# Early stores, roots and loads in a two-sequence encoder kernel, with six of eight gating products per up pair on GpSimd

## The reference, cut to what matters

```python
x = x + 0.5 * swiglu(rmsnorm(x, norm_ffn1), w_ffn1_gate, w_ffn1_up, w_ffn1_down)
x = x + hybrid_mixer(rmsnorm(x, norm_mix), ...)      # attention and gated linear attention
x = x + 0.5 * swiglu(rmsnorm(x, norm_ffn2), w_ffn2_gate, w_ffn2_up, w_ffn2_down)
y = rmsnorm(x, norm_final)

def swiglu(h, w_gate, w_up, w_down):
    return (silu(h @ w_gate) * (h @ w_up)) @ w_down
```

## Time and profile before

| | us |
|---|---|
| median of 3 runs (2459.72 to 2462.23) | 2461.09 |
| the profiled execution | 2464.09 |
| its span, first to last instruction | 2462.3 |
| TensorE busy in it | 2320.7 (94%) |
| VectorE busy | 1190.6 (48%) |
| ScalarE busy | 727.8 (30%) |
| GpSimd busy | 254.1 (10%) |
| mean granted TensorE clock | 0.974 |

### The profile page before, as it was taken

One profiled execution on the slowest core, in us unless ns is written; L12 is line 12 of the kernel. 1 busy time (PEld: TensorE's weight loads), 2 busy tenths in 40 slices (PEclk: granted clock), 3 DMA queues, 4 the chain that ended last, 5 costly groups with the idle time before them and its releaser, 6 DMA issues. The chain is left out here.

```text
span 2462.3 us, 32516 instructions
## 1 busy us (share of the span) xinstructions
PE 2320.7 (94%) x12960; PEld 2011.8 (82%) x12960; DVE 1190.6 (48%) x2022; ACT 727.8 (30%) x1366; POOL 254.1 (10%) x188
## 2 busy tenths in 40 slices
PE   3998999999989999999999889999999999999998
PEld 3998999999968877777778778888888888877887
DVE  5555555555546585856555674511111111136576
ACT  5322222222233344644443211311111111123343
POOL 5000000000000001111001222211111121100000
PEclk7999999999999999999999999999999999999999
DMA  3133222222286565422425824122222222246555
GB/s 121 35 99 100 72 72 73 86 76 72 87 304 219 178 195 151 145 96 83 134 80 171 277 108 159 35 80 81 79 74 72 104 78 89 74 147 198 188 177 174
DMA packets 227191, 298.08 MB, mean 121 GB/s; under 512 B 22880, under 2 KB 141664, under 8 KB 227040
## 3 DMA queue, kind: packets, MB, share of 16 engines
q1 hardware_dynamic: 216672, 275.01, 34.8%
q10 hardware_dynamic: 10368, 20.98, 2.3%
HBM read 205.49 MB, written 87.16 MB: 119 GB/s over the span
## 5 line engine op out<-in xcount | busy, mean ns | idle before, releaser
L1963 PE MATMUL ps<-h_hi,w_hi 128*128 128x512 f32 (+1 forms) x1488 | 536.4, 361 | 5.3 <-ACT q_rot L1139 2.5
L1964 PE MATMUL ps<-h_lo,w_hi 128*128 128x512 f32 (+1 forms) x1488 | 528.7, 355 | 0.0
L1965 PE MATMUL ps<-h_hi,w_lo 128*128 128x512 f32 (+1 forms) x1488 | 528.5, 355 | 0.0
L2030 PE MATMUL ps<-hs,w_hi 128*128 128x384 f32 (+1 forms) x1232 | 391.3, 318 | 50.5 <-DVE u L1530 42.9
L2031 PE MATMUL ps<-hs,w_hi 128*128 128x384 f32 (+1 forms) x1232 | 389.0, 316 | 0.0
L1963 PEld LDWEIGHTS ps<-h_hi,w_hi 128*128 128x128 f32 x1488 | 282.6, 190 | 65.0 <-issue 18.7
L2040 PE MATMUL ps<-w_hi,dh 128*128 128x512 f32 x770 | 304.0, 395 | 18.3 <-DVE w_lo L1596 11.8
L1965 PEld LDWEIGHTS ps<-h_hi,w_lo 128*128 128x128 f32 x1488 | 282.6, 190 | 39.9
L1964 PEld LDWEIGHTS ps<-h_lo,w_hi 128*128 128x128 f32 x1488 | 283.0, 190 | 37.6
L2032 PE MATMUL ps<-hs,w_lo 128*128 128x384 f32 (+1 forms) x992 | 313.0, 316 | 0.0
L2042 PE MATMUL ps<-w_hi,dh 128*128 128x512 f32 x770 | 302.6, 393 | 0.0
(11 more groups left out here) (210 smaller groups left out, 2858.9 us busy)
## 6 DMA issues: line engine op xcount, KB each, us to landing
dr<-hid_mid SPq DMA_DIRECT2D x154, 320.0 KB, 3.1
w_raw<-in_w_ffn_down SPq DMA_DIRECT2D x176, 256.0 KB, 3.4
hid_mid<-st SPq DMA_DIRECT2D x88, 320.0 KB, 3.5
w_raw<-in_w_ffn_gate SPq DMA_DIRECT2D x44, 512.0 KB, 4.0
w_raw<-in_w_ffn_up SPq DMA_DIRECT2D x44, 512.0 KB, 4.8
hid_mid<-sg SPq DMA_DIRECT2D x66, 320.0 KB, 2.6
w_raw<-in_w_in SPq DMA_DIRECT2D x14, 512.0 KB, 4.7
proj<-stage ACTq DMA_DIRECT2D x24, 256.0 KB, 3.2
```

The lines of the kernel that those rows point to most:

```text
L1963: mm(out, hi, rhs_hi, start=first, stop=False)
L1964: mm(out, hi, rhs_lo, start=False, stop=False)
L1965: return mm(out, lo, rhs_hi, start=False, stop=last)
L2030: mm(out, hi[:, k, :], b_hi, start=k == 0 and j in (GP1, GP6, GP5), stop=False, skip_group_check=True)
```

## The change

- GpSimd's order at the start: the roots of tiles 0, 1 and 2, then the splits of tile t followed by the roots of tile t + 3.
- In the up pair, the products for GP5, GP4 and GP3 (six of eight) are made by GpSimd (`g_gate`), with a semaphore of their own; GP2's two, which read PSUM, stay on VectorE.
- SyncE stores each of the three sg blocks when its product is made, behind the two weight loads of that iteration, and each of the four sums when it is made. Two semaphores count them. The SiLU waits for the sg stores and for the making of the sums; the next sums wait for the stores of the sums.
- At the end of gate/up the last four sums come before the last `d_prepare` on VectorE, and SyncE loads a hidden and a weight block for the down stage before the last stores. The same in the second FFN.
- The x tiles are reloaded in every second step, and the gain row later.
- `keep_p1` stands ahead of `d_hi` of the same step on ScalarE. `share_p1` moves to the last five steps of DP2.
- Some semaphores are merged, with counts to match (A2 silu and prod into S, masking into masked).

```diff
@@ -111,7 +111,8 @@
...
-G_MULT = numbered(e for e in GORDER if e[0] % NP in G_OUT and e[0] // NP % 2 == 1)
+G_MULT = numbered(e for e in GORDER if e[0] % NP == GP2 and e[0] // NP % 2 == 1)
+G_GATED = numbered(e for e in GORDER if e[0] % NP in G_OUT[1:] and e[0] // NP % 2 == 1)
@@ -505,16 +506,29 @@
...
-            def store_hidden(f, i):
-                sp.wait_ge(hid_summed, 4 * (GROUPS * f + i + 1))
-                for p, block in ((DP1, hid(f, 0)), (DP2, hid(f, 1)), (DP4, hid(f, 3)), (DP5, ST[f][:, 0, :]),
-                                 (DP6, ST[f][:, 1, :]), (DP7, ST[f][:, 2, :]), (DP3, ST[f][:, 3, :])):
-                    sp.dma_start(hid_mid[p, i], block).then_inc(hid_stored, 16)
+            def store_block(f, i, p, q):
+                sp.dma_start(hid_mid[p, i], hid(f, q)).then_inc(hid_stored, 16)
+
+            def store_hidden(i):
+                up = NP * (2 * i + 1)
+                for p, q, j in ((DP1, 0, GP2), (DP4, 3, GP5), (DP2, 1, GP4)):
+                    if j == GP2:
+                        sp.wait_ge(S["mult"], G_MULT[(up + j, 1)])
+                    else:
+                        sp.wait_ge(S["gated"], G_GATED[(up + j, 1)])
+                    store_block(0, i, p, q)
+
+            def store_sums(f, i):
+                for j, p in enumerate((DP5, DP6, DP7, DP3)):
+                    sp.wait_ge(hid_summed, 4 * (GROUPS * f + i) + j + 1)
+                    sp.dma_start(hid_mid[p, i], ST[f][:, j, :]).then_inc(sums_stored, 16)
 
             def load_hidden(f, n):
                 p, i = divmod(n, GROUPS)
-                if p == 0:
-                    sp.wait_ge(hid_stored, 16 * NP * (GROUPS * f + i + 1))
+                if p in (DP1, DP2, DP4):
+                    sp.wait_ge(hid_stored, 48 * (GROUPS * f + i + 1))
+                else:
+                    sp.wait_ge(sums_stored, 64 * (GROUPS * f + i + 1))
                 if n >= D_HID:
                     sp.wait_ge(W["a_lo"], D_STEPS * f + n - D_HID + 1)
                 sp.dma_start(DR[f][n % D_HID][:, :], hid_mid[p, i]).then_inc(hid_loaded[n % D_HID], 16)
@@ -590,10 +604,12 @@
...
             for q in range(1, G_PAIRS):
                 if q % 2 and q >= 3:
-                    store_hidden(0, q // 2 - 1)
+                    store_sums(0, q // 2 - 1)
                 load_gu1(2 * q + 1)
                 if q + 1 < G_PAIRS:
                     load_gu1(2 * q + 2)
+                if q % 2 == 0:
+                    store_hidden(q // 2 - 1)
@@ -601,9 +617,6 @@
...
-            store_hidden(0, GROUPS - 1)
-            sp.wait_ge(S["done"], len(GORDER))
-            load_gain(gain1[:, :], norm_mix[0:1, :])
@@ -615,9 +628,15 @@
...
-                if 1 <= n <= TT:
-                    sp.dma_start(x_tile(1, n - 1), x_rows(n - 1).rearrange("p (k n) -> p k n", n=P)
-                                 ).then_inc(x_loaded[n - 1], 16)
+                if n == 0:
+                    store_hidden(GROUPS - 1)
+                    store_sums(0, GROUPS - 1)
+                if n % 2 and n // 2 < TT:
+                    t = N1_ORDER[n // 2]
+                    sp.wait_ge(S["done"], len(GORDER))
+                    sp.dma_start(x_tile(1, t), x_rows(t).rearrange("p (k n) -> p k n", n=P)).then_inc(x_loaded[t], 16)
+                if n == 2 * TT:
+                    load_gain(gain1[:, :], norm_mix[0:1, :])
@@ -825,12 +844,19 @@
...
             for v in range(4 * GROUPS):
                 if v % 4 == 1 and v >= 9:
-                    store_hidden(1, v // 4 - 2)
+                    i = v // 4 - 2
+                    sp.wait_ge(S["mult"], len(G_MULT) + 6 * (i + 1))
+                    for p, q in ((DP1, 0), (DP4, 3), (DP2, 1)):
+                        store_block(1, i, p, q)
+                    store_sums(1, i)
                 load_gu2(v)
...
-            store_hidden(1, GROUPS - 2)
+            sp.wait_ge(S["mult"], len(G_MULT) + 6 * (GROUPS - 1))
+            for p, q in ((DP1, 0), (DP4, 3), (DP2, 1)):
+                store_block(1, GROUPS - 2, p, q)
+            store_sums(1, GROUPS - 2)
@@ -838,7 +864,6 @@
...
-            store_hidden(1, GROUPS - 1)
@@ -850,6 +875,11 @@
...
+                if n == 0:
+                    sp.wait_ge(S["mult"], len(G_MULT) + 6 * GROUPS)
+                    for p, q in ((DP1, 0), (DP4, 3), (DP2, 1)):
+                        store_block(1, GROUPS - 1, p, q)
+                    store_sums(1, GROUPS - 1)
                 if n > GROUPS * DP7 and n % 2 and n // 2 - GROUPS * DP7 // 2 - 1 < HT:
@@ -892,12 +922,24 @@
...
-            first_roots(0)
-            first_roots(1)
+            for t in range(3):
+                first_roots(t)
             for t in range(HT):
                 first_t_lo(t)
-                if t + 2 < HT:
-                    first_roots(t + 2)
+                if t + 3 < HT:
+                    first_roots(t + 3)
+            def g_gate(s, c):
+                q, j = divmod(s, NP)
+                lo, hi = (P * x for x in PAIR_CUT[c])
+                if j in G_OUT[1:] and q % 2:
+                    to = hid(0, {GP4: 1, GP3: 2, GP5: 3}[j])[:, lo:hi]
+                    by = {GP5: u3, GP4: p1, GP3: u2}[j][:, lo:hi]
+                    pool.wait_ge(S["silu"], G_SILU[(s - NP, c)])
+                    pool.wait_ge(S["added"], G_ADDED[(s, c)])
+                    nc.gpsimd.tensor_tensor(to, to, by, ALU.mult).then_inc(S["gated"], 1)
+
+            for s, c in GORDER:
+                g_gate(s, c)
@@ -1029,11 +1071,12 @@
                 if j == GP1:
                     act.wait_ge(S["done"], GAT[(s, c)])
                     if q and q % 2 == 0:
-                        act.wait_ge(S["mult"], G_MULT[(s - NP + GP4, c)])
+                        act.wait_ge(S["gated"], G_GATED[(s - NP + GP4, c)])
                     nc.scalar.copy(p1[:, lo:hi], ps[:, Z_BANKS[c], 0:n]).then_inc(S["kept"], 1)
                 elif j in G_OUT and q % 2 == 0:
                     if q and c == 0 and j == GP2:
-                        act.wait_ge(hid_stored, 16 * NP * (q // 2))
+                        act.wait_ge(hid_stored, 48 * (q // 2))
+                        act.wait_ge(hid_summed, 4 * (q // 2))
                     if j == GP2:
@@ -1102,10 +1145,10 @@
                     elif s + D_LEAD + 1 >= G_STEPS:
                         d_hi(0, s + D_LEAD + 1 - G_STEPS)
             for m in range(GROUPS * DP4 + GROUPS - D_TAIL):
+                if m == GROUPS:
+                    keep_p1(0)
                 if m + D_LEAD < D_STEPS and m:
                     d_hi(0, m + D_LEAD)
-                if m == GROUPS:
-                    keep_p1(0)
@@ -1367,9 +1410,10 @@
...
+                    act.wait_ge(hid_stored, 48 * (GROUPS + i))
+                    act.wait_ge(hid_summed, 4 * (GROUPS + i))
                 act.wait_ge(A2["gate"], s + 1)
-                nc.scalar.activation(sg2[:, t, c0:c0 + n], ps[:, GU + 2 * (s % 2), 0:n], ACT.Silu).then_inc(A2["silu"], 1)
+                nc.scalar.activation(sg2[:, t, c0:c0 + n], ps[:, GU + 2 * (s % 2), 0:n], ACT.Silu).then_inc(S["silu"], 1)
@@ -1393,10 +1437,10 @@
                         if i == GROUPS - 1 and t == 1:
                             d_hi(1, c)
             for m in range(GROUPS * DP4 + GROUPS - D_TAIL):
+                if m == GROUPS:
+                    keep_p1(1)
                 if m + D_LEAD < D_STEPS:
                     d_hi(1, m + D_LEAD)
-                if m == GROUPS:
-                    keep_p1(1)
                 t, phase = divmod(m - GROUPS * DP7, 2)
@@ -1526,7 +1570,7 @@
                         if q % 2:
                             dve.wait_ge(S["silu"], G_SILU[last])
                         else:
-                            dve.wait_ge(S["mult"], G_MULT[last])
+                            dve.wait_ge(S["gated"], G_GATED[last])
                     v.tensor_tensor(to[:, part], of, plus[:, part], ALU.add).then_inc(S["added"], 1)
@@ -1534,16 +1578,11 @@
             def g_mult(s, c):
                 q, j = divmod(s, NP)
                 lo, hi = (P * x for x in PAIR_CUT[c])
-                if j in G_OUT and q % 2:
-                    to = hid(0, {GP2: 0, GP4: 1, GP3: 2, GP5: 3}[j])[:, lo:hi]
+                if j == GP2 and q % 2:
+                    to = hid(0, 0)[:, lo:hi]
                     dve.wait_ge(S["silu"], G_SILU[(s - NP, c)])
-                    if j == GP2:
-                        dve.wait_ge(S["done"], GAT[(s, c)])
-                        by = ps[:, Z_BANKS[c], 0:hi - lo]
-                    else:
-                        dve.wait_ge(S["added"], G_ADDED[(s, c)])
-                        by = {GP5: u3, GP4: p1, GP3: u2}[j][:, lo:hi]
-                    v.tensor_tensor(to, to, by, ALU.mult).then_inc(S["mult"], 1)
+                    dve.wait_ge(S["done"], GAT[(s, c)])
+                    v.tensor_tensor(to, to, ps[:, Z_BANKS[c], 0:hi - lo], ALU.mult).then_inc(S["mult"], 1)
 
             def hid_sums(f, i, which):
                 a11, a12, a21, a22 = (hid(f, q) for q in range(4))
```

(32 more changed lines are left out.)

23 lines of the change are left out of this document (11 added, 12 removed).

## The result

The changed kernel takes 2368.37 us (median of 4 runs, 2367.24 to 2370.87); the kernel before, timed beside it, 2461.37. The ratio is 0.9624, with a 95% interval of 0.9608 to 0.9641: 92.5 us or 3.8% less. The forecast was 2361, with a range of 2351 to 2383. The profiled execution took 2369.3 with a span of 2367.5, so the span fell by 94.8 us; the sum had 100.4. TensorE's granted clock, as a mean of the span, rose from 0.974 to 0.989.

The account below looks back on a forecast made before the run. TensorE's queue bounds the kernel, winnable in its pauses and the slow clock behind each. 62.7 + 13.4 + 7.1 + 8.0 + 9.8 - 0.6 = 100.4 us off, giving 2360.7 by the median, taken as 2361; range 2351 to 2383.

Parts of the forecast that it names:

- Stores and waits of gate/up: First FFN's gate/up: earlier stores and up load remove ten group pauses and the low clock behind; 62.7 us, bounds 36 and 63.
- The rival with a late up load: Gate/up: the up load's flight stays 6.1 us, so each group pauses 0.6 us or more; 2367 to 2388, chance 0.20.
- Six products on GpSimd: Gate/up's up pair: gating products moved off VectorE, nothing on the path; 0 us, bounds 0 and 4.
- The rival of GpSimd and VectorE in each other's way: Gate/up: products on GpSimd hold VectorE, splits and products later; 1 us a group, 10 us, 2371, chance 0.05.
- grown splits: Gate/up sign of being wrong: VectorE's 0.68 us splits grown beside the GpSimd products.
- Roots at the start: Start: roots ahead of splits on GpSimd end VectorE's idle, second token part at 60.5, not 73.85; 13.4 us, bounds 5.7 and 14.
- the rival's 8: Start: only the first wait is freed, 8 instead of 13.4 us; with down stages 12 instead of 24.9, 2379, chance 0.08.
- followed through with the same durations: Start: queues followed with unchanged durations; scales of tiles 2, 3, 4 at 20.2, 29.0, 37.6, second token part at 60.5.
- Into the down products: Start of both down stages: hidden loads before stores, sums before last d_prepare; 7.1 us and 8.0 us, bounds 4 and 16.
- keep_p1: Second product of both down stages: copying tiles ahead of d_hi ends TensorE's wait; 6.2 + 3.6 us, bounds 6.6 and 10.
- share_p1: Last five DP2 steps, beside DP5 preparation: later adds make an eviction 0.3 us late; cost 0.3 us, twice, bounds 0 and 2 each.

## Why the prediction was right, and where it was not

- **Stores and waits of gate/up: 62.7, measured 62.5 as a stage and 60.5 by undoing.** The chain held at each link: the up load about 1 us after the fourth sum; its data used 4.4 us after issue one group earlier (313.19 to 317.55), forecast 4.6; no pause behind it; clock 1.00. SyncE's order and the SiLU's wait were undone together, so their shares are open. The rival with a late up load needed 6.1 us of flight and fell.
- **Six products on GpSimd: 0, measured 0.** Their lengths are 1.01 and 0.74 us; I had taken 1.0 and 0.7.
- **The rival of GpSimd and VectorE in each other's way was real, at another place.** I looked for it only at the new products and priced it there. There it lengthens splits by 0.5 us, which nobody waits for, and 11 groups of it cost nothing. The prediction had named grown splits as a sign of being wrong; they came, and no time with them. The rule of the Trainium skill, GPSIMD Engine Reference, section Key points, which the prediction weighed there, holds: the trace agrees, 0.69 us alone and 1.20 beside a product. But the change also made the scales and GpSimd's old splits meet at the start, and there VectorE sets the end.
- **Roots at the start: 13.4, measured 9.4 (9.1 by undoing, 7.1 by the times).** That is nearer to the rival's 8 than to the forecast. The step that failed is "followed through with the same durations". The two scales of a tile grew by 1.7 us together, and behind the first pair two more instructions by 1 each; GpSimd's four splits by 1 to 2.4. The order in the sum was right, the lengths in it were those of instructions that had never met. This is 4.0 of the 5.6 us that the sum is off. That the growth comes of the two engines meeting is shown, by the kernel that measures them and by the one without GpSimd's splits; that it is all of the 4.0 is argued from the slip of the scales, since the kernel without those splits on GpSimd put them on VectorE instead.
- **Into the down products: 15.1; and keep_p1: 9.8.** Their sum with share_p1's cost, 24.3, is what the stages gained, 24.5, but not by the steps named. The reordering to which I gave the first is worth 0 and at most 3.8 us; the rows point at the one-by-one stores and the sg stores already out, which I had put under gate/up, and at the gain load behind them. keep_p1's is worth 4.3 to 7.8: 2.2 to 3.9 in the second FFN, where 3.6 was forecast, and 2.1 to 3.9 in the first, where it was 6.2, since there 2.3 us or more of the old wait was an echo of the late start. The causes overlap: once one is cured, the other has less to give, and undoing them singly adds up to less than the whole. That the sum came out within 0.2 us is in part luck.
- **share_p1: 0.3 twice as cost, measured 0.9 to 1.0 twice.** The waits are the 0.6 us that the working came near; the rest is not in a wait.
- **The output projection became 1.8 us longer**, in code that isn't changed, and the rows don't put it down to the change. From its first matmul to the first gate product behind its last transposes it takes 184.5 us before and 186.2 after, and in the profiles of the eleven variants, with the same code there, between 184.0 and 187.3. With the start this makes up the 5.6 us. In one 25 us stretch the clock is 0.87, before 0.93, with about as much work:

```profile
1360.30:1385.30 25.00, 20.29 (x122) 16.94 (x123) 20.20 (x36) 4.47 (x7) 9.08 (x5) 0.87 0.08 27
```
```profile
1445.30:1470.30 25.00, 20.55 (x130) 17.00 (x127) 21.48 (x40) 4.47 (x7) 8.93 (x5) 0.93 0.08 27
```

  The first row is after, the second before. Pauses of TensorE stand in both (11.2 and 10.5 us of waits for x2a); why the clock came out lower after is open.
- **The range** was added up wrongly: every bound at its good end is 63 + 14 + 16 + 10 = 103 us, and with 5 us for the run this gives 2353 and not 2351. The result lies inside either.

## What to carry to other kernels

Where a pause comes once per group, look first at what one in-order queue issues between two needs: here stores stood ahead of a load and a SiLU waited for them, and changing that was worth 60 us, while moving arithmetic to an idle engine was worth nothing. When a reordering lets two engines work at the same time that never did before, don't reuse their lengths: measure a pair. And when two cures aim at one stage, price them together, then undo both singly and jointly; the sum can be right with its parts wrong. Last, a stage's length comes from one execution, with that execution's clock: see where it lies among the times of its kernel, and compare a stage that the edit doesn't touch, before you read a difference of 2 us in it.

## What the runs showed of the hardware

- A GpSimd product of 512 columns and a VectorE instruction with two SBUF inputs take turns: VectorE 0.72 to 1.69 us (512 columns), 1.26 to 2.22 (1024), 1.31 to 2.22 (scalar_tensor_tensor, 1024).
- A VectorE instruction with one SBUF input was held up just as much: tensor_scalar on 1024 fp32 columns, which ran at 0.72 us (twice the rate of the two-input one), took 1.69.
- PSUM with SBUF input: 0.72 us beside GpSimd as alone.
- A pause of TensorE of 1.98 us, at the same place in the same code, was followed by 20 us at a granted clock of 1.00 in one execution and at 0.92 in another; that is 1.7 us of the stage.
- GpSimd pays as well: twelve products of 512 columns took 16.02 us beside PSUM readers, 17.97 beside the 512-column kind and 21.17 beside the 1024-column kind.
